# Two-block transformer kernel: seven early modulation products moved from TensorE to VectorE, and the start of the first projection reordered

## The chip, the cores and the metric

The kernel runs on one core of one Trainium2 chip. The metric is the device time of one execution in microseconds (us), lower is better. Before the change it is 2683.89 us, the median of three runs (2682.54 to 2684.22).

## The reference, cut to what matters

Two transformer blocks run one after the other on x of 256 tokens by 2048 features, all in float32. The change touches only the beginning of the first block, the modulation that comes from a conditioning vector c:

```python
c_act = jax.nn.silu(c)                         # (1, 2048)
mod = c_act @ w_ada[l] + b_ada[l]              # w_ada is 2048 x 12288
sh1, sc1, gt1, sh2, sc2, gt2 = jnp.split(mod, 6)
h = rms_norm(x, g_norm1) * (1 + sc1) + sh1
proj = h @ w_in[l]                             # first projection
```

`c_act @ w_ada` is a product of one row with a large matrix: there is little arithmetic in it, and 100 MB of weights to load. `sh1` and `sc1` are needed before the first projection can be multiplied, for each block of 128 features of h.

## The kernel before, in words

**Weights and units.** A weight load brings 512 rows by 512 columns (1 MB) into one of four `raw` buffers. Each load is used in two units (`DU`), 1024 values per partition each. For a unit, ScalarE copies its half of the load to `w_hi` in the reduced format fp32r (L1135), VectorE subtracts that from the original into `w_lo` (L1657), and TensorE makes 12 matmuls of 128x512 (L632): hi times hi, lo times hi, hi times lo, over two blocks of features and two blocks of tokens. Both helper engines run a `split` ahead of TensorE: at unit u they split unit u + 3 (`AHEAD` is 3). `w_hi` and `w_lo` have four buffers (`SPL`), so that ScalarE's split of unit u waits for TensorE's unit u - 4.

**Modulation loads.** The products with `w_ada` that feed `sh1` and `sc1` come in 32 loads of 1 MB (`NPRO`), numbered a = 0 to 31, called p0 to p31 here as products and e0 to e31 as loads. They go through a ring of four buffers of their own (`PRO_RING`): two in `early_mix`, two in `wide`. p0 to p15 (`LEAD` is 16) form two groups of eight, and are multiplied before unit 0, in `prologue()`; they give the first eight blocks of features. p16 to p31 form four groups of four loads: sh1 and sc1 for blocks 8 to 11 (p16 to p19, p20 to p23), and for blocks 12 to 15 (p24 to p27, p28 to p31). Every product is four TensorE matmuls (L662) whose stationary operand is 32 columns of `ccol`, of which the first holds silu(c) and the rest are zero. The sums of a group gather in a PSUM bank, VectorE copies them to `part` (L1708, or L1703 for the first two groups), TensorE adds up the partitions with a column of ones (`part_columns`, L679, L676 for the first two), and VectorE adds the bias and the gain (L1726, L1730, L1733). When sh1 and sc1 of a segment are there, ScalarE scales the transposed x (L1254) and VectorE splits it in `actT_hi` and `actT_lo` (L1910, L1911, the function `modulated`), two blocks of features at a time; q0 to q7 name these pieces. TensorE's unit u of the first eight needs piece q = u for u up to 3, with every piece shared by the three output groups.

**Order.** Every engine runs a program of its own in a fixed order. `prologue()` lists the steps before unit 0; before the change they end with products p16 and p17. `modulation(u)` lists what follows unit u: first the columns of the group that the product before finished, then the product p(17 + u), for u from 1 to 14. VectorE does in its unit u: `split` of unit u + 3, attention stages, then the events of `modulation(u)`, then pieces of h. So anything that VectorE does for p(17 + u) stands behind its split of unit u + 3, and that split stands behind the arrival of the weight load of unit u + 3. The columns of a group come behind unit 3 (p16 to p19), 7, 11 and 15.

**Queues.** SyncE issues all the weight loads in order. After each of the first eight projection loads w0, w1, ... it issues two modulation loads (w0, e16, e17, w1, e18, e19, ...). A modulation load waits until the product four before it has been made (`early_ada`, L485): for TensorE's product that is the semaphore `ada_used`, or `part_ready` when it was the last of its group. A projection load waits until the split of the load four before it is made (L455). GpSimd's queue waits for all six groups (`part_ready` at 6) and then loads the table of attention biases, 1.5 MB, over the two ring buffers in `wide` (L1614). TensorE turns that table with matmuls at L779 (`mirror`), the first behind unit 17.

Of the kernel before, what the change touches and what calls it, by code (L numbers as in the profile page):

```python
# [9 lines left out]
ALU = mybir.AluOpType  # L10
# [7 lines left out]
NW = 512  # L18
UC = 2
DU = 2  # L20
RAW = 4
SPL = 4
AHEAD = 3
# [40 lines left out]
LEAD = 2 * SEGMENTS[0][1]  # L64
NPRO = 32
PRO_RING = 4
# [12 lines left out]
LOAD_OF = [(g, r) for g, (kind, k0, n) in enumerate(GROUPS) for r in range(n)]  # L79
# [5 lines left out]
def last_of_group(a):  # L85

    return LOAD_OF[a][1] == GROUPS[LOAD_OF[a][0]][2] - 1


def completed(a):  # L90

    if a < WIDE:
        return [LOAD_OF[a][0]] if last_of_group(a) else []
    return [len(GROUPS) + (a - WIDE) // 4] if a % 4 == 3 else []


def sums_by(a):

    if a < NPRO:
        return LOAD_OF[a][0] + 1  # L100
    return len(PROLOGUE) + ((a - NPRO) // 2 + 1 if a < WIDE else (WIDE - NPRO) // 2 + a + 1 - WIDE)
# [8 lines left out]
def prologue():  # L110

    steps = [("diagonal",)]
    for a in range(LEAD):
        steps.append(("part", a))
        if a >= 1:
            steps += [("columns", n) for n in completed(a - 1)]
        if 5 <= a < 13:
            steps.append(("x", 2 * (a - 5)))
        if a == 13:
            steps.append(("gains",))  # L120
        if a == 14:
            steps.append(("rows",))
    steps += [("columns", n) for n in completed(LEAD - 1)]
    return steps + [("part", LEAD), ("part", LEAD + 1)]


def modulation(u):

    def products(v):

        after = [0, 1] if v == 0 else [v // DU + 1]
        return [NPRO + LOADS_A.index(k) for j in after if v >= 0 and v % DU == 0 and j < len(LOADS_W) - 1
                for k in range(LOADS_W[j] + 1, LOADS_W[j + 1])]

    def early(v):

        return [LEAD + 1 + v] if 0 < v < NPRO - LEAD - 1 else []
    events = [("row", n) for a in products(u - 3) for n in completed(a) if n >= len(GROUPS)]  # L140
    events += [("columns", n) for a in products(u - 2) for n in completed(a)]
    events += [("columns", n) for a in early(u - 1) for n in completed(a)]
    return events + [("part", a) for a in early(u) + products(u)]


def takes_bank(what, n_):

    return what != "part" or (NPRO <= n_ < WIDE and n_ % 2 == 0) or (LEAD <= n_ < NPRO and LOAD_OF[n_][1] == 0)


def banks_of(u):

    return len([1 for e in modulation(u) if takes_bank(*e)])
# [49 lines left out]
def build(nc, A, out, scr_bias, scr_x):  # L203
    ctx = ExitStack()
    with ctx:
        def sb(name, shape, dt=F32, c=ctx):
            return c.enter_context(nc.sbuf_tensor(name, shape, dt))

        def sem(name):
            return ctx.enter_context(nc.semaphore(name))  # L210
# [38 lines left out]
        part = sb("part", [P, NW])  # L249
# [17 lines left out]
        ccol = sb("ccol", [P, DC, 32])  # L267
# [27 lines left out]
        early = [early_mix[:, 0, :], early_mix[:, 1, :], wide[:, 0, :], wide[:, 1, :]]  # L295
# [12 lines left out]
        early_in = [sem(f"early_in{i}") for i in range(PRO_RING)]  # L308
# [30 lines left out]
        part_ready = sem("part_ready")  # L339
# [6 lines left out]
        c_ready = sem("c_ready")  # L346
        col_ready = sem("col_ready")
        ada_used = sem("ada_used")
        lam_exp = sem("lam_exp")
        xb_in = sem("xb_in")  # L350
        gt_in = sem("gt_in")
# [83 lines left out]
        def _(sp):  # L435
# [36 lines left out]
            def early_ada():  # L472

                a = asked[0]
                asked[0] += 1
                if a >= PRO_RING:
                    used = a - PRO_RING
                    if used < LEAD:
                        sp.wait_ge(ada_used, used + 1)
                    elif last_of_group(used):  # L480
                        sp.wait_ge(part_ready, sums_by(used))
                    else:
                        sp.wait_ge(ada_used, used + 1 - (LOAD_OF[used][0] - 2))
                view, width = columns_of(a)
                sp.dma_start(early[a % PRO_RING].rearrange("p (k n) -> p k n", n=width), view) \  # L485
                    .then_inc(early_in[a % PRO_RING], 16)
# [116 lines left out]
        def _(pe):  # L603
# [38 lines left out]
            def part_sums(a):  # L642


                if a < NPRO:
                    src = early[a % PRO_RING]
                    pe.wait_ge(early_in[a % PRO_RING], 16 * (a // PRO_RING + 1))
                else:
                    ld = LOADS_A[a - NPRO]
                    src = raw[:, ld % RAW, :]  # L650
                    pe.wait_ge(raw_in[ld % RAW], L.landed(ld))
                g, r = LOAD_OF[a]
                n_ = GROUPS[g][2]
                if a < LEAD:
                    dst = acc[2][:, g, :]
                begins, ends = (r == 0, r == n_ - 1) if a < NPRO else (a % 2 == 0, a % 2 == 1)
                if a >= LEAD:
                    if begins:
                        opened[0], _ = wait_bank()
                    dst = bank[opened[0]]  # L660
                for j in range(4):
                    ins = pe.matmul(dst[32 * j:32 * j + 32, :], ccol[:, 2 * r + j // 2 if n_ == 8 else 4 * r + j, :],  # L662
                                    src[:, j * NW:(j + 1) * NW], start=begins, stop=ends)
                if a >= LEAD and ends:
                    ins.then_inc(bank_full[opened[0]], 1)
                elif a < NPRO:
                    ins.then_inc(ada_used, 1)
# [95 lines left out]
            b, _ = wait_bank()  # L763
# [130 lines left out]
            for w in range(24, 28):  # L894
# [3 lines left out]
                m = L.n[("acc", pair)]  # L898
# [5 lines left out]
                for c in range(2):  # L904
                    for t in range(TT):
                        for s, (x, wt) in enumerate(((0, w_hi), (0, w_lo), (1, w_hi))):
                            ins = pe.matmul(acc[pair][:, t, :], MIXT[x][:, 12 + c, t * P:(t + 1) * P],  # L907
                                            wt[:, (u0 + c) % SPL, p * NW:(p + 1) * NW], start=c == 0 and s == 0,
                                            stop=c == 1 and s == 2)
# [732 lines left out]
        def _(dve):  # L1642
            L = Ledger()

            def link(ins):

                ins.then_inc(dch, 1)
                dve.wait_ge(dch, L.next("dch"))

            def split():  # L1650

                u = L.n.get("split", 0)
                if u >= UNITS:
                    return
                ld = LOADS_W[u // DU]
                dve.wait_ge(hi_ready, L.next("split"))
                dve.tensor_tensor(w_lo[:, u % SPL, :], raw[:, ld % RAW, (u % DU) * 1024:(u % DU + 1) * 1024],  # L1657
                                  w_hi[:, u % SPL, :].bitcast(F32), ALU.subtract).then_inc(lo_ready, 1)
# [34 lines left out]
            def part_sums(a):  # L1693

                g, r = LOAD_OF[a]
                if takes_bank("part", a):
                    opened[:] = L.n["bank"] % 2, L.n["bank"] // 2 + 1
                    L.n["bank"] += 1
                if (a < NPRO and not last_of_group(a)) or (a >= NPRO and a % 2 == 0):
                    return  # L1700
                if a < LEAD:
                    dve.wait_ge(ada_used, a + 1)
                    ins = dve.tensor_copy(part[:, :], acc[2][:, g, :])  # L1703
                else:
                    b = opened[0]
                    dve.wait_ge(bank_full[b], opened[1])
                    if a < NPRO or r == 1:
                        ins = dve.tensor_copy(part[:, :], bank[b][:, :])  # L1708
                    else:
                        ins = dve.tensor_tensor(part[:, :], part[:, :], bank[b][:, :], ALU.add)  # L1710
                ins.then_inc(part_ready, 1)
                dve.wait_ge(part_ready, sums_by(a))
                if a >= LEAD:
                    dve.sem_inc(bank_free[b], 1)
# [157 lines left out]
            for c in range(4):  # L1872
                ins = dve.memset(sel[32 * c:32 * c + 32, c % 2:c % 2 + 1], 1.0)
            link(ins)
            b = next_bank()
# [3 lines left out]
            b = next_bank()  # L1879
# [35 lines left out]
            def turned():  # L1915
# [3 lines left out]
            todo_of = {"part": part_sums, "columns": part_columns, "diagonal": lambda: diagonal(inv_rms()),  # L1919
                       "x": lambda k: turned(), "gains": gain_columns, "rows": second_rows}  # L1920
            for s in prologue():
                if s[0] in todo_of:
                    todo_of[s[0]](*s[1:])
            for _ in range(DU):
                split()
            modulated(0)
            for _ in range(AHEAD - DU):
                split()
            for q in pieces_of(1)[1:]:
                modulated(q)  # L1930
# [177 lines left out]
            for g in range(4):  # L2108
# [12 lines left out]
                for t in range(TT):  # L2121
                    ins = dve.tensor_tensor(s3[:, t, :], s3[:, t, :], grow[:, cols], ALU.mult)
# [276 lines left out]
            r = x_inv_rms()  # L2399
            link(dve.tensor_copy(r_mlp, r[:, 0:TT]))  # L2400
            dve.sem_inc(r_last, 1)
            for t in range(TT):
                dve.scalar_tensor_tensor(out=x_res[:, t, 3 * NW:D], in0=x_res[:, t, 3 * NW:D], scalar=r_mlp[:, t:t + 1],
                                         in1=grow[:, 3 * NW:D], op0=ALU.mult, op1=ALU.mult).then_inc(y_ready, 1)
# [50 lines left out]
```

## Time and profile before

| what | value |
|---|---|
| median of three runs | 2683.89 us (2682.54 to 2684.22) |
| the profiled execution's own time | 2680.39 us |
| span of its trace | 2678.6 us |
| TensorE matmuls busy | 2604.9 us, 97% of the span, 12160 matmuls |
| VectorE busy | 1549.4 us, 58% |
| ScalarE busy | 1167.9 us, 44% |
| DMA | 561.73 MB, mean 210 GB/s, 391 and 379 GB/s in the first two fortieths |
| granted TensorE clock, whole span | 0.991 of full speed |

The time outside the span is 1.8 us. The matmul ends in this profile are modelled and overlap each other, so that a busy share near 100% says that TensorE had a matmul in flight, not that it ran at its peak. Starts are the better measure: the distance between the first matmuls of two units is what a unit costs.

### The profile page before, as it was taken

Reading aid. Unit: us, or ns where it says so; the run is one execution under the profiler, and the core shown is the slowest. Engines: PE = TensorE matmul, PEld = TensorE weight load, DVE = VectorE, ACT = ScalarE, POOL = GpSimd, SP = SyncE. Lnnn points to the kernel's source line nnn. Section 1 sums busy time; section 2 is a strip of 40 time slices with the busy share of each in tenths; the row PEclk is TensorE's granted clock in tenths of the full one; section 3 lists DMA queues with packets and bytes.
Section 4 is the critical chain, followed back from the end, with each engine's and each line's share of the span. In section 5 each row is a group of like instructions: output and inputs, shape, how many; then the busy total and the mean of one; then the engine's idle time right before and its main releaser. Section 6 shows DMA issues by size and latency. Waiting matters only on the chain.

```text
span 2678.6 us, 32964 instructions
## 1 busy us (share of the span) xinstructions
PE 2604.9 (97%) x12160; PEld 2084.3 (78%) x12160; DVE 1549.4 (58%) x1706; ACT 1167.9 (44%) x1522; POOL 53.5 (2%) x86
## 2 busy tenths in 40 slices
PE   6999989899999999999999999999999999999997
PEld 2676766688888888887888877888888888888886
DVE  1456654667776555557655454556556565656565
ACT  2344553344434444444544445444444444444443
POOL 1010110000000000000000000000000000000000
PEclk8999999999999999999999999999999999999999
DMA  9967766657776555555655544656565555555553
GB/s 391 379 235 283 259 252 220 219 194 244 244 245 233 189 188 188 189 192 170 218 189 187 173 144 145 205 202 217 189 203 189 188 188 188 188 188 188 189 187 109
DMA packets 262882, 561.73 MB, mean 210 GB/s; under 512 B 9250, under 2 KB 13556, under 8 KB 261900
## 3 DMA queue, kind: packets, MB, share of 16 engines
q1 hardware_dynamic: 260688, 549.25, 60.6%
q0 software_dynamic: 1728, 9.19, 1.0%
q10 hardware_dynamic: 380, 2.13, 0.2%
q8 instruction: 56, 0.92, 0.1%
q14 instruction: 30, 0.25, 0.0%
HBM read 556.32 MB, written 4.21 MB: 209 GB/s over the span
## 4 chain that ended last, share of the span: by engine, by line
PE 83%; DVE 2%; ACT 1%; issue 1%; DMA 0%; POOL 0%; DVEq 0%; POOLq 0%; ACTq 0%
PE acc L632 78%; PE bank L715 2%; PE bank L662 1%; PE bank L864 1%; DVE w_lo L1657 0%; PE acc L855 0%; PE acc L1064 0%; PE acc L854 0%; PE acc L1063 0%; PE acc L907 0%; PE bank L727 0%; DMA raw<-in_w_ada 0%; PE bank L689 0%; DVE wide L2173 0%; DVE x_res L2177 0%
## 5 line engine op out<-in xcount | busy, mean ns | idle before, releaser
L1657 DVE TENSOR_TENSOR w_lo<-raw,w_hi 128x1024 fp32r<-128x1024 f32 x852 | 1037.9, 1225 | 828.6 <-ACT w_hi L1135 799.9
L1135 ACT ACTIVATE w_hi<-raw 128x1024 fp32r<-128x1024 f32 x852 | 901.2, 1060 | 1063.2 <-PE acc L632 958.6
L632 PE MATMUL acc<-w_hi,actT_hi 128*128 128x512 f32 (+1 forms) x2112 | 832.7, 394 | 1.4 <-DVE actT_lo L1792 1.0
L632 PE MATMUL acc<-w_hi,actT_lo 128*128 128x512 f32 (+1 forms) x2112 | 820.9, 389 | 0.0
L632 PE MATMUL acc<-w_lo,actT_hi 128*128 128x512 f32 (+1 forms) x2112 | 820.3, 388 | 0.0
L632 PE MATMUL acc<-w_hi,mixT_hi 128*128 128x512 f32 (+1 forms) x1280 | 504.4, 394 | 8.8 <-DVE mixT_lo L1782 4.3
L632 PE MATMUL acc<-w_hi,mixT_lo 128*128 128x512 f32 (+1 forms) x1280 | 499.1, 390 | 0.0
L632 PE MATMUL acc<-w_lo,mixT_hi 128*128 128x512 f32 (+1 forms) x1280 | 498.3, 389 | 0.0
L632 PEld LDWEIGHTS acc<-w_hi,actT_hi 128*128 128x128 f32 x2112 | 397.1, 188 | 106.3 <-issue 20.0
L632 PEld LDWEIGHTS acc<-w_hi,actT_lo 128*128 128x128 f32 x2112 | 396.9, 188 | 82.5
L632 PEld LDWEIGHTS acc<-w_lo,actT_hi 128*128 128x128 f32 x2112 | 397.3, 188 | 79.3 <-issue 1.0
L632 PEld LDWEIGHTS acc<-w_hi,mixT_hi 128*128 128x128 f32 x1280 | 241.4, 189 | 69.4 <-issue 11.4
L632 PEld LDWEIGHTS acc<-w_hi,mixT_lo 128*128 128x128 f32 x1280 | 241.4, 189 | 49.6
L632 PEld LDWEIGHTS acc<-w_lo,mixT_hi 128*128 128x128 f32 x1280 | 241.8, 189 | 47.6
L2150 DVE TENSOR_TENSOR x_res<-x_res,acc 128x1024 f32<-128x1024 f32 x68 | 83.1, 1221 | 30.4 <-PE acc L632 30.4
L662 PE MATMUL bank<-raw,ccol 128*32 128x512 f32 x384 | 47.2, 599 | 6.4 <-DMA raw<-in_w_ada 4.0
L715 PE MATMUL bank<-cst,work 128*128 128x128 f32 x356 | 47.7, 273 | 5.5 <-DVE att L2013 2.5
L2150 DVE TENSOR_TENSOR wide<-wide,acc 128x1024 f32<-128x1024 f32 x36 | 44.0, 1221 | 14.5 <-PE acc L632 14.5
L1183 ACT ACTIVATE mixT_hi<-bank 128x512 fp32r<-128x512 f32 (+1 forms) x54 | 25.6, 503 | 61.2 <-PE bank L715 37.4
L715 PEld LDWEIGHTS bank<-cst,work 128*128 128x128 f32 x356 | 41.6, 140 | 13.7 <-DVE att L2013 2.9
L1439 ACT ACTIVATE work<-acc,kpe 128x512 f32<-128x512 f32 x48 | 30.4, 686 | 39.3 <-PE acc L632 39.3
L1686 DVE SCALAR_TENSOR_TENSOR part<-raw,ccol,part 128x512 f32<-128x512 f32 x60 | 45.1, 751 | 1.7
(269 smaller groups left out, 1063.1 us busy)
## 6 DMA issues: line engine op xcount, KB each, us to landing
raw<-in_w_ff SPq DMA_DIRECT2D x128, 1024.0 KB, 5.1
raw<-in_w_in SPq DMA_DIRECT2D x108, 1024.0 KB, 5.1
raw<-in_w_ada SPq DMA_DIRECT2D x64, 1024.0 KB, 5.2
raw<-in_w_gate SPq DMA_DIRECT2D x44, 1024.0 KB, 5.0
raw<-in_w_up SPq DMA_DIRECT2D x44, 1024.0 KB, 5.1
raw<-in_w_down SPq DMA_DIRECT2D x44, 1024.0 KB, 5.0
early_mix<-in_w_ada SPq DMA_DIRECT2D x16, 1024.0 KB, 9.2
wide<-in_w_ada SPq DMA_DIRECT2D x16, 1024.0 KB, 8.9
```

The costliest lines, as they stand in the source:

```text
L632: last_mm = pe.matmul(acc[p][:, t, 0:width], act[x][:, k0 + c, t * P:(t + 1) * P], w[:, u % SPL, c * NW:c * NW + width], start=first and c ...
L662: ins = pe.matmul(dst[32 * j:32 * j + 32, :], ccol[:, 2 * r + j // 2 if n_ == 8 else 4 * r + j, :], src[:, j * NW:(j + 1) * NW], start=beg ...
L715: ins = pe.transpose(bank[b][:, j * P:(j + 1) * P], src_of(j), ident)
L864: ins = pe.matmul(bank[b][:, 0:S], v[:, k, h * P:(h + 1) * P], attT[:, k, :], start=(k == 0), stop=(k == 1))
L1135: act.activation(w_hi[:, u % SPL, :], raw[:, ld % RAW, (u % DU) * 1024:(u % DU + 1) * 1024], ACT.Copy) \
L1183: act.activation(dst, bank[b][:, 0:n], ACT.Copy).then_inc(bank_hi, 1)
L1439: ins = act.activation(stg[:, t * NW:(t + 1) * NW], acc[p][:, t, :], ff, scale=scale[:, t:t + 1])
L1657: dve.tensor_tensor(w_lo[:, u % SPL, :], raw[:, ld % RAW, (u % DU) * 1024:(u % DU + 1) * 1024], w_hi[:, u % SPL, :].bitcast(F32), ALU.subt ...
L1686: ins = dve.scalar_tensor_tensor(out=part[:, :], in0=src, scalar=ccol[:, k, 0:1], in1=part[:, :], op0=ALU.mult, op1=ALU.add)
L2150: link(dve.tensor_tensor(dst[:, :, g * NW:(g + 1) * NW], dst[:, :, g * NW:(g + 1) * NW], acc[g % 2][:, :, :], ALU.add))
```

## The change

Three things are done.

- **Seven products go to VectorE.** The second and third product of each of the four groups of four, except p17, are made on VectorE: p18, p21, p22, p25, p26, p29 and p30. Each is four instructions over 128x512: the load's quarter times a column of `ccol`, added to `part`. The first of a group's VectorE products begins with a plain `tensor_scalar`, which sets `part`; the others are `scalar_tensor_tensor`. TensorE makes the first and the last product of a group in its bank (and p17), and when the last is made, VectorE adds the bank to `part` instead of copying it. A new semaphore `dve_used` tells SyncE that a load multiplied on VectorE can be overwritten.
- **p17 is moved** from before unit 0 to behind unit 0.
- **The first split on VectorE is moved** ahead of the columns of the second group (the last thing that unit 0 waits for), and the second split behind the first piece of h, which it stood ahead of.

```diff
@@ prologue
     steps += [("columns", n) for n in completed(LEAD - 1)]
-    return steps + [("part", LEAD), ("part", LEAD + 1)]
+    return steps + [("part", LEAD)]
@@ modulation
-        return [LEAD + 1 + v] if 0 < v < NPRO - LEAD - 1 else []
+        return [LEAD + 1 + v] if 0 <= v < NPRO - LEAD - 1 else []
...
+def on_dve(a):
+
+    return LEAD + 1 < a < NPRO and LOAD_OF[a][1] in (1, 2)
+
+
+def released_by(a):
+
+    if last_of_group(a) and a >= LEAD:
+        return "part_ready", sums_by(a)
+    return ("dve_used" if on_dve(a) else "ada_used",
+            len([b for b in range(a + 1) if on_dve(b) == on_dve(a) and not (b >= LEAD and last_of_group(b))]))
@@ SyncE, early_ada
-                    used = a - PRO_RING
-                    if used < LEAD:
-                        sp.wait_ge(ada_used, used + 1)
-                    elif last_of_group(used):
-                        sp.wait_ge(part_ready, sums_by(used))
-                    else:
-                        sp.wait_ge(ada_used, used + 1 - (LOAD_OF[used][0] - 2))
+                    name, m = released_by(a - PRO_RING)
+                    sp.wait_ge({"part_ready": part_ready, "ada_used": ada_used, "dve_used": dve_used}[name], m)
@@ TensorE, part_sums
+                if on_dve(a):
+                    return
@@ VectorE, part_sums
+                if on_dve(a):
+                    dve.wait_ge(early_in[a % PRO_RING], 16 * (a // PRO_RING + 1))
+                    for j in range(4):
+                        src, col = early[a % PRO_RING][:, j * NW:(j + 1) * NW], ccol[:, 4 * r + j, 0:1]
+                        if j == 0 and not on_dve(a - 1):
+                            ins = dve.tensor_scalar(part[:, :], src, col, None, ALU.mult)
+                        else:
+                            ins = dve.scalar_tensor_tensor(out=part[:, :], in0=src, scalar=col, in1=part[:, :],
+                                                           op0=ALU.mult, op1=ALU.add)
+                        link(ins)
+                    dve.sem_inc(dve_used, 1)
+                    return
...
-                    if a < NPRO or r == 1:
+                    if a >= NPRO and r == 1:
                         ins = dve.tensor_copy(part[:, :], bank[b][:, :])
                     else:
                         ins = dve.tensor_tensor(part[:, :], part[:, :], bank[b][:, :], ALU.add)
@@ VectorE, before unit 0
             for s in prologue():
+                if s == ("columns", 1):
+                    split()
                 if s[0] in todo_of:
                     todo_of[s[0]](*s[1:])
-            for _ in range(DU):
-                split()
             modulated(0)
-            for _ in range(AHEAD - DU):
+            for _ in range(AHEAD - 1):
                 split()
```

## Rows read from the trace of the kernel before

**Rows 1.** Windows: instructions busy by engine, granted clock, DMA share, GB/s.

```profile
51.00:53.00 2.00, 1.09 (x8) 0.20 (x8) 0.82 (x4) 0.00 (x0) 0.00 (x0) 0.69 1.05 409
...
100.00:110.00 10.00, 10.00 (x52) 6.39 (x50) 5.61 (x9) 4.67 (x5) 0.00 (x0) 1.00 1.05 401
```

**Rows 2.** Waits of TensorE from 60 to 150 us: total, times, longest.

```profile
PE bank L662 <- DMA early_mix<-in_w_ada: 0.6, 1, 0.6
```

**Rows 3.** ScalarE's timeline: start, duration, instruction, count, idle before and its releaser.

```profile
57.29 1.09 ACT L1254 ACTIVATE xT<-xT,mcol 128x256 f32<-128x256 f32 x2 [0.81 <-DVEq L1742]
...
77.68 2.01 ACT L1135 ACTIVATE w_hi<-raw 128x1024 fp32r<-128x1024 f32 x2 [5.73 <-DMA raw<-in_w_in]
...
95.89 2.08 ACT L1254 ACTIVATE xT<-xT,mcol 128x256 f32<-128x256 f32 x4 [1.73 <-DVEq L1742]
...
108.54 1.06 ACT L1135 ACTIVATE w_hi<-raw 128x1024 fp32r<-128x1024 f32 x1 [3.67 <-DMA raw<-in_w_in]
...
117.05 1.06 ACT L1135 ACTIVATE w_hi<-raw 128x1024 fp32r<-128x1024 f32 x1 [5.79 <-DMA raw<-in_w_in]
```

**Rows 4.** TensorE's timeline at the start of unit 0 and of unit 1.

```profile
59.60 1.94 PE L662 MATMUL bank<-early_mix,ccol 128*32 128x512 f32 x8 [0.61 <-DMA early_mix<-in_w_ada]
61.47 0.79 PE L632 MATMUL acc<-w_hi,actT_hi 128*128 128x512 f32 x1
...
65.45 0.39 PE L632 MATMUL acc<-w_hi,actT_hi 128*128 128x512 f32 x1
...
66.15 0.39 PE L632 MATMUL acc<-w_hi,actT_hi 128*128 128x512 f32 x1
...
68.99 1.07 PE L662 MATMUL bank<-wide,ccol 128*32 128x512 f32 x8
```

**Rows 5.** TensorE's timeline, first matmuls of units 4 and 5, and the columns.

```profile
76.80 0.95 PE L679 MATMUL bank<-ones,part 128*128 128x1 f32 x8
...
78.67 0.50 PE L632 MATMUL acc<-w_hi,actT_hi 128*128 128x512 f32 x1
...
82.61 0.50 PE L632 MATMUL acc<-w_hi,actT_hi 128*128 128x512 f32 x1
...
93.37 0.95 PE L679 MATMUL bank<-ones,part 128*128 128x1 f32 x8
...
109.94 0.95 PE L679 MATMUL bank<-ones,part 128*128 128x1 f32 x8
...
126.51 0.95 PE L679 MATMUL bank<-ones,part 128*128 128x1 f32 x8
132.90 1.02 PE L779 MATMUL bank<-wide,att 128*128 128x512 f32 x2
```

**Rows 6.** VectorE's timeline at the first units.

```profile
59.62 0.42 DVE L1910 CAST actT_hi<-xT 128x512 fp32r<-128x512 f32 x1
...
65.07 0.69 DVE L1911 TENSOR_TENSOR actT_lo<-xT,actT_hi 128x512 fp32r<-128x512 f32 x1
...
71.03 2.36 DVE L1657 TENSOR_TENSOR w_lo<-raw,w_hi 128x1024 fp32r<-128x1024 f32 x2 [2.00 <-ACT w_hi L1135]
```

**Rows 7.** VectorE's timeline where it makes other modulation products later on.

```profile
588.88 0.48 DVE L1684 TENSOR_SCALAR part<-raw,ccol 128x512 f32<-128x512 f32 x1
...
591.85 2.36 DVE L1657 TENSOR_TENSOR w_lo<-raw,w_hi 128x1024 fp32r<-128x1024 f32 x2
594.12 3.11 DVE L1686 SCALAR_TENSOR_TENSOR part<-raw,ccol,part 128x512 f32<-128x512 f32 x4
```

**Rows 8.** DMA issues by tile: count, KB each, median us from issue to landing.

```profile
raw<-in_w_in SPq DMA_DIRECT2D x108, 1024.0 KB, 5.1
...
wide<-in_w_ada SPq DMA_DIRECT2D x8, 1024.0 KB, 8.9
```

**Rows 9.** The load of the bias table: its issue, and its time to landing.

```profile
124.78 1.00 POOL L1614 DMA_DIRECT2D wide<-bias_by_distance  x1 [103.49 <-DVE part L1708]
...
DMA to landing us min/median/max: 7.7/7.7/7.7
```

More of the change, by code:

```diff
@@ L348, in build @@
         ada_used = sem("ada_used")
+        dve_used = sem("dve_used")
         lam_exp = sem("lam_exp")
```

## Prediction, made before the changed kernel was run

> **What bounds the kernel now.** The whole program is bound by TensorE, but the change acts only in the first 135 us, so I read that stretch alone, first by windows. While the 32 modulation loads run, TensorE has work in flight all the time and the DMA engines are also full, with a share of 1.05 [rows 1]. Two things are at their limit together, and the question is which one is just ahead. TensorE's waits say that TensorE is the later: from 60 to 150 us it waited 0.6 us in all [rows 2]. ScalarE's timeline shows the other side: its `w_hi` waits for the arrival of weights, at 77.68 and 108.54, four loads later, so a projection load and its two modulation loads arrive every 7.72 us, 2.57 us each [rows 3]. TensorE's starts give its own beat: unit 1 takes 68.99 - 66.15 = 2.84 us [rows 4], unit 4 with p21 behind it 82.61 - 78.67 = 3.94, so a product costs 1.10, and columns come every 16.57 us or four units (93.37, 109.94, 126.51) [rows 5], 8.28 per pair of units. TensorE is thus only 0.56 us per pair slower than the DMA, and its data lie ready a little longer with each pair.
>
> **What the change removes.** Seven products at 1.10 us make 7.7 us off TensorE. If nothing else bound it, that would be the gain.
>
> **The start.** Before: unit 0 begins at 61.47, when p17 is through [rows 4]. After: p16 ends at 59.60 - 0.61 = 58.99 [rows 4], ScalarE has piece q0 at 57.29 + 1.09 = 58.38 [rows 3], and VectorE splits it in 0.42 + 0.69 [rows 6] right then, since two w_lo splits no longer stand ahead (now it starts at 59.62, behind them). Unit 0 starts at about 59.6, 1.8 us earlier. The split moved ahead of the columns costs nothing: it runs beside TensorE's column matmuls, and if it came late the columns would be late by a part of its 1.2 us. But unit 1 needs q1, whose lo part ends at 65.07 + 0.69 = 65.76 [rows 6]: it comes behind ScalarE's copy of the second load, which waits for DMA, and nothing in the change moves it. Unit 0 at the slow clock takes some 4.7 us, p17 1.1, and unit 1 starts at 65.85 against 66.15. The start gives 0.3 us; p17 is hidden in the gap. Unit 2 would follow p18 at 69.98; without p18 it starts at 68.65, unit 3, behind p19, at 72.5, and TensorE wants the first columns at 75.3.
>
> **What VectorE adds, and where it stands.** A group's first VectorE product takes 591.85 - 588.88 = 2.97 us, the other, all `scalar_tensor_tensor`, 3.11 and a link, 3.2; a split 1.15, half the step from 591.85 to 594.12 [rows 7]; the add of the bank 0.69, as the copy before it and as the tensor_tensor of its shape [rows 6]. Four of the one and three of the other: 21.5 us on an engine that is busy for 5.6 us in ten there [rows 1]. In sum there is room. In order there is less: VectorE's product behind unit u stands behind its split of unit u + 3, that waits for the weight's arrival, and the group's columns on TensorE wait for all of it. Followed group by group (each time is the one before it plus a duration above; a load's split starts 1.1 us behind its arrival):
>
> - *First columns.* Split of unit 4 at 71.03 as now [rows 6], p18 72.2 to 75.15, split of unit 5 to 76.35, add to 77.05. Columns at 77.15, against 76.80 before [rows 5]. TensorE waits 1.8 us: the gain is gone, +0.35.
> - *Second.* TensorE goes on from 77.15, skips p21 and p22 and wants the columns at 91.45. VectorE: p21 81.5 to 84.5; the next load arrives at 77.68 + 7.72 = 85.4, its split ends 87.65; p22 to 90.85, split to 92.0, add to 92.7. Columns at 92.8 against 93.37: -0.55.
> - *Third.* TensorE wants them at 107.15. VectorE: ScalarE's pieces q4 and q5 go ahead of its next copy as now, 95.89 to 97.97 [rows 3], so the split of unit 11 ends at 100.1; p25 to 103.1, pieces q4, q5 to 105.4, split of unit 12 to 106.55, p26 to 109.8, split to 110.95, add to 111.65. Columns at 111.75 against 109.94: +1.8, and TensorE has waited 4.6 us.
> - *Fourth.* TensorE wants them at 111.75 + 1.87 + 2.84 + 2.84 + 3.94 + 2.84 = 126.1. Here the ring matters. SyncE may issue e29 only when p25 is made, 103.1, against about 99 now, and e30 when p26 is, 109.8 against 103. A load takes at least 5.1 us from issue to landing [rows 8]. e29 lands at 108.3, 2.4 us behind its place in the queue, w7 at 110.9 (now 108.54), e30 at 114.9, e31 at 117.4, w8 at 120 (now 117.05 [rows 3]). Splits of unit 16 to 122.3, p30 to 125.5, split to 126.65, add to 127.35. Columns at 127.45 against 126.51: +0.95.
>
> *A page's figure for that latency.* The Trainium skill, DMA: Bandwidth & Descriptors, section on the anatomy of one DMA, has a fixed part of about 2.0 us and the bytes at 436 GB/s. That would be 4.4 us for 1 MB in place of the row's 5.1, and the fourth columns 0.7 us earlier, a minor shift, but on its side the late release costs less.
>
> **What is late last.** GpSimd loads the bias table when all groups are made: 124.78 now [rows 9], some 2.9 us later after, 127.65. It takes 7.7 us to land [rows 9], so 135.4. TensorE's first matmul on it stands at 132.90 now [rows 5], in the same microsecond in which the table lands (124.78 + 7.7 = 132.5). After, TensorE would be there at 127.45 + 0.82 + 2 x 2.84 = 133.9 and wait for the table to 135.4: **+2.5 us**. Beyond that TensorE is bound by itself, nothing gives slack back, and the shift reaches the end. The other end of this case: if the ring's late releases cost nothing, w8 arrives as now, the sixth group is done at 124.5 and the table at 132.5, so -0.4; if each is late by another microsecond, +4.
>
> Sum: 2680.39 + 2.5 = 2682.9 for an execution like the profiled one, which lies 3.5 us under the median of 2683.89; put to the median, 2686.4. A difference of this kernel under about 0.2% (5.4 us) can't be told from no change.
>
> **Rivals.**
>
> 1. *The gain is whole.* If VectorE is never what the columns wait for, TensorE has 7.7 + 0.3 = 8.0 us less: 2675.9. For it: VectorE's busy share, and that TensorE is the later now. Against: the DMA is only 0.56 us per pair behind it, and the order above. Chance 0.05.
> 2. *Waits and covers come out even.* The columns wait less than I count (a link is cheaper, a load comes a little earlier), and the table lands as now. Then the time is that of the table's landing, between 0 and 3 us less: 2682.5. Chance 0.21.
> 3. *The DMA queue runs dry* (slower). Place: SyncE's wait for `dve_used`, with w7, e30, e31 and w8 queued behind it. It decides if a load released late needs not 5.1 but the 8.9 us that ring loads take now [rows 8]. Then e29 lands at 112, w7 114.6, e30 118.7, w8 123.8, p30 is made at 130.2, the last add ends at 132, the table lands at 140: +7.1, 2691.0. For: the DMA is full, other loads stand ahead. Against: the 8.9 is mostly queue, and a late release is late because the queue is empty. Chance 0.12.
> 4. *The clock falls in the new waits.* At 51 to 53 us, with TensorE idle between small products, the granted clock goes to 0.69 of full on the mean, the lower of its levels (1.2 of 2.4 GHz) for part of it [rows 1]; in unit 0 nine matmuls take 65.45 - 61.47 = 3.98 us instead of 2.1 [rows 4] until it is back. A wait of 4.6 us could do the same: 1.9 us a time. Behind the third columns the fourth wait (1.35 us) and that for the table (1.5 us) take this up; only if it happens at two or more of the waits does it show, +2 to +4 on the forecast, 2689.5. Chance 0.07.
>
> The Trainium skill, TensorE: Matmul & The Clock Gate, section on why this matters for your kernels, warns of just such idle gaps between bursts of matmuls, as dropping the clock to half. By that rule the fourth rival would happen at least at the third columns; the trace has such a drop only at 51 us.
>
> **How the numbers follow.** The forecast, +2.5 us, has 0.55; the rivals 0.05, 0.21, 0.12 and 0.07. Forecast alone: 2683.5 to 2688. The range of 8 in 10 takes in the second and fourth and most of the third: 2680 to 2691. Faster by over 0.2%: the first rival and a little of the second, 0.06. Slower by over 0.2% (over 2689.3): two thirds of the third, a third of the fourth, 0.10. Within 0.2%: 0.84.
>
> **What would show it.** TensorE's waits, 60 to 150 us, should have columns (L679 before) waiting for VectorE's add of the bank: 1.8, 1.4, 4.6 and 1.4 us. Unit 0 should start near 59.6 and unit 1 near 65.8. SyncE should wait for the products on VectorE, and the DMA share should have a dip near 104 us. The first L779 matmul should start near 135.4, right after the table's landing, and everything later keep that distance. The prediction is wrong if that matmul starts before 130 (then VectorE and DMA had slack I did not see) or after 138, or if a shift made here changes again later, for instance through a wait at a modulation load in the attention stages.

## The result, and the profile after

The changed kernel takes 2690.82 us, the median of nine runs (2688.91 to 2695.24), beside 2682.72 us for the kernel before (nine runs, 2681.04 to 2685.63). The ratio is 1.0031, 95% interval 1.0022 to 1.0040: slower by about 8 us, where the forecast was 2.5 us slower and 0.84 of the chance lay within 5.4 us of no change. The profiled execution of the changed kernel is at its median (span 2688.8 us); that of before was 2.3 us under what is now the median of before, so the two spans differ by 10.2 us and the times by 8.1.

TensorE's timeline of the changed kernel, at the rows that answer to [rows 4, 5]; an idle time before the row and its releaser stand in brackets:

```profile
59.67 0.79 PE L641 MATMUL acc<-w_hi,actT_hi 128*128 128x512 f32 x1 [0.71 <-DVE actT_lo L1934]
...
66.28 0.50 PE L641 MATMUL acc<-w_hi,actT_hi 128*128 128x512 f32 x1
...
76.92 1.05 PE L690 MATMUL bank<-ones,part 128*128 128x1 f32 x8 [0.96 <-DVE part L1733]
...
94.09 1.05 PE L690 MATMUL bank<-ones,part 128*128 128x1 f32 x8 [1.19 <-DVE part L1733]
...
113.08 1.68 PE L690 MATMUL bank<-ones,part 128*128 128x1 f32 x8 [3.02 <-DVE part L1733]
...
130.45 0.95 PE L690 MATMUL bank<-ones,part 128*128 128x1 f32 x8
139.64 1.14 PE L790 MATMUL bank<-wide,att 128*128 128x512 f32 x2 [2.64 <-DMA wide<-bias_by_distance]
```

The start is as forecast, 1.8 us earlier for unit 0 and nothing for unit 1. The matmuls on the columns (L690, four times) stand 0.1, 0.7, 3.1 and 3.9 us later than before, the first matmul on the bias table 6.7 us later. TensorE waits at three of the columns, for VectorE's add of the bank, and at the table; at the fourth columns, where 1.4 us were forecast, it does not wait. VectorE's timeline in front of the first columns shows what stands in one row behind an arrival: a split, p18, a split, the add.

```profile
70.91 1.23 DVE L1668 TENSOR_TENSOR w_lo<-raw,w_hi 128x1024 fp32r<-128x1024 f32 x1 [2.13 <-ACT w_hi L1146]
72.05 0.48 DVE L1712 TENSOR_SCALAR part<-wide,ccol 128x512 f32<-128x512 f32 x1
72.57 2.33 DVE L1714 SCALAR_TENSOR_TENSOR part<-wide,ccol,part 128x512 f32<-128x512 f32 x3
75.04 1.22 DVE L1668 TENSOR_TENSOR w_lo<-raw,w_hi 128x1024 fp32r<-128x1024 f32 x1
76.18 0.68 DVE L1733 TENSOR_TENSOR part<-part,bank 128x512 f32<-128x512 f32 x1
```

The weight loads show where the extra lateness comes from. SyncE's timeline (start, time, issue, count) and ScalarE's (`w_hi` behind the arrivals of w3, w4 and w8):

```profile
74.98 2.28 SPq L494 DMA_DIRECT2D wide<-in_w_ada  x2
77.31 0.51 SPq L469 DMA_DIRECT2D raw<-in_w_in  x1
79.03 5.58 SPq L494 DMA_DIRECT2D early_mix<-in_w_ada  x2
...
111.14 2.28 SPq L494 DMA_DIRECT2D wide<-in_w_ada  x2
```

```profile
77.53 2.00 ACT L1146 ACTIVATE w_hi<-raw 128x1024 fp32r<-128x1024 f32 x2 [5.71 <-DMA raw<-in_w_in]
86.72 2.01 ACT L1146 ACTIVATE w_hi<-raw 128x1024 fp32r<-128x1024 f32 x2 [7.18 <-DMA raw<-in_w_in]
...
122.88 2.22 ACT L1146 ACTIVATE w_hi<-raw 128x1024 fp32r<-128x1024 f32 x2 [8.24 <-DMA raw<-in_w_in]
```

e22 could be issued at 74.98 only (70.1 before), when p18 was made on VectorE. Behind it stood e23, which waits for the group's sum: the two issues together last till 77.26, past VectorE's add at 76.18. By their times to landing e22 arrives at 80.8, 0.6 us later than before, and e23 at 84.2, 1.4 us later: most of the lateness of w4, the load behind them, comes with e23. Between w3 and w4 now lie 9.2 us; the beat before was 7.72 [rows 3]. w5, w6 and w7 arrive 1.6, 2.6 and 4.1 us later than before, and w8 at 122.88 against 117.05, 5.8 us. The table follows:

```profile
130.50 1.00 POOL L1625 DMA_DIRECT2D wide<-bias_by_distance  x1 [109.77 <-DVE part L1733]
...
DMA to landing us min/median/max: 9.1/9.1/9.1
```

And three windows in which TensorE waited or ran at the lower clock, their entries in the order of [rows 1]:

```profile
70.00:80.00 10.00, 9.04 (x48) 5.71 (x47) 7.00 (x9) 3.83 (x4) 0.00 (x0) 0.96 1.02 356
...
110.00:120.00 10.00, 6.98 (x25) 4.57 (x25) 8.02 (x11) 2.00 (x2) 0.00 (x0) 0.67 0.96 331
...
140.00:150.00 10.00, 10.00 (x33) 7.10 (x32) 2.65 (x3) 4.35 (x6) 0.00 (x0) 0.83 0.51 177
```

The DMA moves 356 GB/s at 70 to 80 us and 331 at 110 to 120, where it moved 408 and 400. The granted clock falls behind each of TensorE's four waits in the rows above: 0.67 of full on the mean at 110 to 120, 0.83 at 140 to 150. The step on GpSimd that stood at 142.70 before stands at 151.12, 8.4 us later: 6.7 from the table and 1.7 from the clock behind it. From that step to the end of the span it is 2535.9 us before and 2537.7 here. Among the traces of the experiments this remainder goes from 2536.1 to 2542.1, so a single span says little about a few us.

### The profile page after: what moved, and what is told of

It reads as the page before. It is cut to its first block, busy times and chain, and to the rows that moved or that the text cites. A ratio compares the mean times of both kernels' runs of the same rounds, so it can differ in the third digit from the quotient of the medians.

```text
span 2688.8 us, 32887 instructions
## 1 busy us (share of the span) xinstructions
PE 2608.4 (97%) x12104; PEld 2089.2 (78%) x12104; DVE 1568.3 (58%) x1734; ACT 1167.6 (43%) x1522; POOL 54.0 (2%) x86
## 4 chain that ended last, share of the span: by engine, by line
PE 89%; DMA 4%; DVE 4%; ACT 2%; issue 1%; POOL 0%; SPq 0%; DVEq 0%; POOLq 0%; ACTq 0%
PE acc L641 82%; PE bank L726 2%; DMA raw<-in_w_in 2%; PE bank L673 1%; DMA wide<-in_w_ada 1%; DMA raw<-in_w_ada 1%; DVE w_lo L1668 1%; PE bank L875 1%; ACT w_hi L1146 1%; DVE part L1714 0%; PE acc L866 0%; PE acc L1075 0%; DMA wide<-bias_by_distance 0%; PE acc L865 0%; PE acc L1074 0%
```

## The experiments

Every version was run beside the kernel before on the same chip, 5 to 11 times. The ratio to the kernel before has its 95% interval in brackets; 0.001 is 2.7 us. The changed kernel stands at 1.0031. "At 143 us" is the lateness of GpSimd's first step behind the modulation stage, against the trace of before. Such a lateness, like every start quoted below, is from one execution per version. "..." marks what a diff leaves out.

### Which part of the change

**The start alone.** `on_dve` is false for all, and the last product's sum is copied as before.

```diff
-    return LEAD + 1 < a < NPRO and LOAD_OF[a][1] in (1, 2)
+    return False
```

> Only the new start: p17 behind unit 0, first split ahead of the columns; all 32 products on TensorE. Theory A (VectorE's order and the ring's late releases cause the loss): the start is worth nothing, unit 1 begins near 66.2 as in both kernels, and the time is that of before, 2682.7 within 1 us. Rival B (the start itself costs, because e21 is issued 4 us later and everything behind it in SyncE's queue with it): the DMA share dips near 75 us and the time is 2684.5 to 2687.

Measured: 1.0002 (0.9993 to 1.0012), +0.3 at 143 us, w4 at 85.13, w8 at 117.22. The later issue of e21 costs nothing.

**The products alone.** The start of before (p17 ahead of unit 0, two splits behind the columns), the seven products on VectorE.

```diff
-    return steps + [("part", LEAD)]
+    return steps + [("part", LEAD), ("part", LEAD + 1)]
...
-        return [LEAD + 1 + v] if 0 <= v < NPRO - LEAD - 1 else []
+        return [LEAD + 1 + v] if 0 < v < NPRO - LEAD - 1 else []
```

> Only the seven products on VectorE, with the start of before. Theory A: nearly the whole loss, 2689 to 2692, first columns at 76.9 us, first matmul on the bias table near 139.5. Rival B (the start is to blame for a good part): 2684 to 2687.

Measured: 1.0031 (1.0018 to 1.0043), first matmul on the table at 141.21, w8 at 124.47. The whole loss is in the products.

### Order, amount of work, release

**The product ahead of the split.** Same work, other order in VectorE's unit.

```diff
             def unit(todo=()):
+                events = modulation(L.n.get("unit", 0))
+                for e in events:
+                    if e[0] == "part" and e[1] < NPRO and on_dve(e[1]):
+                        part_sums(e[1])
                 split()
...
```

> The changed kernel, but VectorE makes its product of a unit ahead of that unit's split instead of behind it. Same work, same engines, other order. Theory A: p18 is made from 68.8 to 71.8 in a gap, e22 is issued at 71.8 instead of 75, no columns wait but the third (3.7 us), the table is issued near 123 and the first matmul on it is near 131.4 (before: 132.9, changed: 139.6): 2680.5 to 2683. Rival E (it is VectorE's amount of work or the port to its memory, not the order): 2688 to 2691.

Measured: 0.9996 (0.9987 to 1.0005), no loss left; the interval lies wholly under that of the changed kernel. VectorE's timeline and ScalarE's:

```profile
69.10 0.48 DVE L1718 TENSOR_SCALAR part<-wide,ccol 128x512 f32<-128x512 f32 x1
69.61 2.33 DVE L1720 SCALAR_TENSOR_TENSOR part<-wide,ccol,part 128x512 f32<-128x512 f32 x3
72.09 2.36 DVE L1668 TENSOR_TENSOR w_lo<-raw,w_hi 128x1024 fp32r<-128x1024 f32 x2
```

```profile
85.35 2.01 ACT L1146 ACTIVATE w_hi<-raw 128x1024 fp32r<-128x1024 f32 x2 [5.69 <-DMA raw<-in_w_in]
...
117.35 1.06 ACT L1146 ACTIVATE w_hi<-raw 128x1024 fp32r<-128x1024 f32 x1 [6.89 <-DMA raw<-in_w_in]
```

p18 is made in a gap in which VectorE waited for a load; e22 goes out at 72.03, and w4 and w8 come when they came before. VectorE makes as many products, for as long each, so neither its amount of work nor a slower access to its memory was the loss. TensorE still waits 3.3 us at the third columns (108.41), and the first matmul on the table is at 132.25, forecast 131.4. At 143 us this version is 0.5 us early.

**Work on VectorE that nobody reads.** All products are TensorE's, and VectorE does the same 28 instructions on constants in the same places.

```diff
+                    idle = probs[:, 0:2, :].rearrange("p a s -> p (a s)")
...
+                            ins = dve.tensor_scalar(idle, src, col, None, ALU.mult)
...
+                            ins = dve.scalar_tensor_tensor(out=idle, in0=src, scalar=col, in1=idle,
...
```

> The new start, all 32 products on TensorE with the ring released by TensorE, and on VectorE, in the places of the seven products, the same 28 instructions on constants and a scratch tile, whose result nobody reads. It holds VectorE's order alone, without late releases and without TensorE's gain. Theory A: the third columns are 1 to 2 us late, loads keep their 7.7 us beat (arrivals of w4 and w8 near 85.4 and 117.2), time 1 to 2.5 us over the kernel before: 2684.5 to 2686. Rival F (VectorE's order is most of the loss, the ring little): 2688 to 2691.

Measured: 1.0014 (1.0005 to 1.0022), 3.8 us, more than forecast. w4 at 85.77 and w8 at 119.85: the beat was not kept to the end. What is late in this version too is VectorE's copy of a group's sum, which releases the group's last buffer; that this is the cause was not tried by itself. At 143 us +3.6.

**The same, with the late release.** SyncE waits for VectorE's place too.

```diff
+                    if late(a - PRO_RING):
+                        sp.wait_ge(dve_used, len([b for b in range(a - PRO_RING + 1) if late(b)]))
```

> As the run with idle products, but SyncE waits in addition for VectorE's place before it reuses the buffer, as in the changed kernel. The difference to that run is the late release alone. Theory A: w4 arrives near 86.8 to 88.5 and w8 near 122 to 124, the table is issued near 130.5, time 6 to 9 us over the kernel before, 2689 to 2692. Rival F: within 1.5 us of the run with idle products.

Measured: 1.0021 (1.0012 to 1.0029), 1.9 us over the one before by the ratios, whose intervals overlap. Its one trace has w4 at 87.03, w8 at 123.41, the table at 140.02 and +8.9 at 143 us; it belongs to the slowest of its eleven runs, and behind 143 us that run is another 4.2 us longer than the trace of before. The arrivals show the mechanism; how many us the release alone costs stays between 2 and 5.

**Four products instead of seven**, in the changed kernel's order.

```diff
+    return LEAD + 1 < a < NPRO and LOAD_OF[a][1] in (1, 2) and a not in (22, 26, 30)
```

> The changed kernel in its own order, but only one product of a group on VectorE (p18, p21, p25, p29); p22, p26, p30 back on TensorE. Theory A (two products, a split between them, and the add in one chain behind each load's arrival): only p18 is still in the way, w4 arrives near 86.7, but the second to fourth columns no longer wait; the table is issued near 124.5 and the time is that of before within 1.5 us. If the loss goes by the number of products: 4/7 of 8 us, 2688 to 2689.

Measured: 1.0013 (1.0004 to 1.0022), +3.5 us, under the 4/7 of the loss but not the zero that I forecast. The columns do come back, 94.15, 110.36 and 125.81 (before: 93.37, 109.94, 126.51). But w4 at 87.40 and w8 at 121.70 stay late, and the table, issued at 126.05, is used at 135.72 after a wait of 3.29 us. The columns were not the whole path.

### The clock

**Idle matmuls in the waits.** TensorE multiplies constants into the bank that the next real matmul overwrites, once with 2, 2, 6 and 5 of them and once with 1, 1, 3 and 3.

```diff
+                if n_ in WARM:
+                    b, _ = wait_bank()
+                    for _ in range(WARM[n_]):
+                        pe.matmul(bank[b][:, :], ident, cst[:, 0:NW], start=True, stop=True)
                 pe.wait_ge(part_ready, L.value("groups", sums_of(n_), 4))
...
```

> The changed kernel with idle matmuls (identity times constants, into the bank that the next real matmul overwrites) in front of the columns' and the table's waits: 2, 2, 6 and 5 of them, about 0.5 us each, so that TensorE is busy while it waits. Theory A: the waits stay, the granted clock stays at full, and only the half-clock stretch behind the last wait (the table's) and part of that behind the third columns come off the end: 1.5 to 3.5 us less than the changed kernel, 2687.3 to 2689.3. Rival C (the clock is the loss, the waits by themselves are covered): 2683 to 2685. Rival D (the clock costs nothing at the end): 2690 to 2692.

Measured: 1.0041 (1.0027 to 1.0054). The matmuls took 0.86 us each, not 0.5, ran past the waits, and made all later. The try had no verdict on the clock.

> The changed kernel with idle matmuls again, but cut to the waits that its own trace shows: 1, 1 and 3 ahead of the first three columns and 3 ahead of the table (0.86 us each, as measured in the first try, where they ran past the waits and made everything later). If the half-clock stretches are part of the loss at the end: full clock from 70 to 150 us, first matmul on the table still near 139.6, everything behind it 1.7 us earlier than in the changed kernel, 2687.5 to 2690 where the changed kernel gives 2691. If they are not: 2690.5 to 2692.5.

Measured: 1.0037 (1.0024 to 1.0051), beside 1.0031 (1.0018 to 1.0043) for the changed kernel, run again beside it:

> The changed kernel once more, beside the others on the same chip, as what they are compared with: 7.5 to 9 us over the kernel before, first matmul on the table 6.5 to 8.5 us later than in the kernel before.

TensorE's windows with idle matmuls (busy, granted clock, DMA share, GB/s):

```profile
80.00:90.00 10.00, 10.00 (x48) 1.00 1.04 385
90.00:100.00 10.00, 8.40 (x43) 1.00 1.01 351
...
110.00:120.00 10.00, 7.26 (x25) 0.69 0.94 326
120.00:130.00 10.00, 10.00 (x47) 0.97 1.00 385
130.00:140.00 10.00, 9.98 (x43) 1.00 0.83 287
140.00:150.00 10.00, 9.74 (x37) 1.00 0.56 188
```

The clock stays up at the first, second and last wait, of which 0.79, 1.60 and 0.28 us were left, and falls at the third, where 2.74 us were left. The columns stand where they stood (93.76, 113.45, 130.86), and at 143 us the kernel is 7.5 us late; the repeated changed kernel, whose wait at the table was 0.87 us in that execution, is 7.4 late. So here a half-clock stretch ahead of another wait cost nothing that shows, and the one behind the table is there in some executions only: in the repeated one the clock fell behind a wait of 1.82 us at the fourth columns instead. I have no gain from a kept clock to show. In both versions' traces the excess over the changed kernel arises behind 143 us (6.2 and 5.3 us more than in the trace of before, against 1.8 for the changed kernel); why is open.

### The table

**Its use one unit later.**

```diff
-            todo = {-7: [("mirror", 0)], -6: [("mirror", 1)], -5: [("qk", 0), ("mirror", 2)], -4: [("mirror", 3)],
+            todo = {-6: [("mirror", 0)], -5: [("qk", 0), ("mirror", 1)], -4: [("mirror", 2)],
...
```

> The changed kernel with each of the six steps on the bias table one unit later. Theory A: TensorE has unit 18 to do while the table arrives at 139.6, so the wait of 2.7 us goes, and with it the stretch at half the clock (1.7): 4 us less than the changed kernel, 2686 to 2688. Rival G (the shift is made before the table, by the columns): no more than 1 us less.

Measured: 1.0023 (1.0014 to 1.0032), 2 us less than the changed kernel. At 143 us it is 5.0 late instead of 8.4, but behind the attention stages, at GpSimd's step that stood at 380.68 before, 9.0 where the changed kernel is 9.8. Why most of the gain goes again between was not found.

**Its load issued by SyncE**, behind w9, instead of by GpSimd.

```diff
+                    if n[0] == 10 and i is None:
+                        sp.wait_ge(brow_out, 16)
+                        sp.wait_ge(part_ready, len(PROLOGUE))
+                        sp.dma_start(biasE, bass.AP(scr_bias.tensor, 0, [[1, P], [512, H], [1, 384]])) \
+                            .then_inc(bias_in, 16)
...
-            pool.wait_ge(part_ready, len(PROLOGUE))
-            pool.dma_start(biasE, bass.AP(scr_bias.tensor, 0, [[1, P], [512, H], [1, 384]])).then_inc(bias_in, 16)
```

> The changed kernel with only the table's load moved to SyncE behind w9. If the table's landing is a term of its own in the loss: it lands near 137 instead of 139.6, TensorE does not wait for it nor drop its clock behind it, 3 to 4.4 us less than the changed kernel, 2686 to 2688. If the shift is all made by the columns and releases ahead of it: no more than 1 us less, 2690 to 2691.

Measured: 1.0021 (1.0012 to 1.0030), 2.7 us less by the ratios, whose intervals overlap; at 143 us the kernel is 5.7 late instead of 8.4, the same 2.7. The table lands in 6.4 us and TensorE uses it at 138.55 without a wait. Taken so, the table is a term of its own, about a third of the loss, and two thirds are made ahead of it. The edit does one thing more: SyncE now waits for the sixth group before it issues w10, and the DMA is at 158 GB/s from 120 to 130 us, where it was at 366; TensorE does not wait for a weight load behind it.

### What the idea is worth

**All modulation events ahead of the split**, in VectorE's units 0 to 14.

```diff
             def unit(todo=()):
-                split()
+                ahead = L.n.get("unit", 0) <= 14
+                if not ahead:
+                    split()
...
+                if ahead:
+                    split()
+                    run(todo)
```

> The changed kernel, but in VectorE's units 0 to 14 all that belongs to the modulation (products, the add of the bank, the columns) stands ahead of the split. Theory A: the third columns move from 108.4 (products alone ahead) to about 107, the fourth to about 121.5, the table is issued near 119 and the first matmul on it is near 128: 2678 to 2680.5, 4 to 5 us under the kernel before. Rival H (a split that stands behind TensorE's product now holds up a unit, or the loads' beat is what ends last): 2682 to 2685.

Measured: 0.9992 (0.9983 to 1.0001). Third and fourth columns at 106.61 and 122.40, table used at 129.56, 3.2 us early at 143 us. That trace is of the shortest of its eleven executions; the ratio stands for about 2 us, half of the 4 to 5 forecast. TensorE still waits 3 us at the third columns.

**The same with five products**, p26 and p30 back on TensorE.

```diff
-    return LEAD + 1 < a < NPRO and LOAD_OF[a][1] in (1, 2)
+    return LEAD + 1 < a < NPRO and LOAD_OF[a][1] in (1, 2) and a not in (26, 30)
```

> The version with all modulation events ahead of the split, and p26 and p30 given back to TensorE, so that VectorE makes five products. In the version with seven TensorE waited 3 us at the third columns. Here that wait should go for 1.1 us of matmuls, and the third columns come near 105, the table is issued near 118.5, first matmul on it near 127.5: 1 to 2 us under the version with seven, 2677 to 2680.5. If the loads' beat or the table ends last in both, no difference: 2680 to 2682.

Measured: 0.9992 (0.9983 to 1.0001), no further gain, and the trace shows why. TensorE's timeline:

```profile
104.59 0.95 PE L690 MATMUL bank<-ones,part 128*128 128x1 f32 x8
...
119.94 0.95 PE L690 MATMUL bank<-ones,part 128*128 128x1 f32 x8
129.80 2.07 PE L790 MATMUL bank<-wide,att 128*128 128x512 f32 x2 [3.32 <-DMA wide<-bias_by_distance]
```

No columns wait any more, the fourth come at 119.94, 6.6 us earlier than before [rows 5]. The table is issued at 119.51, but now takes 10.2 us, with weight loads of SyncE in flight beside it (one issued about 4 us ahead of it, one about 1 us behind). TensorE waits 3.3 us, its clock is at 0.71 in the window from 130 to 140 us, and at 143 us the 6.6 us are 0.1. This trace is of one of the two longest executions of eleven, 4.7 us over their median, and behind 143 us it is 5.1 us longer than that of before, so it shows where the gain can go, not how much goes on the mean.

**Five products, the table used later**, by the diff of "Its use one unit later".

> The five-product version with each step on the bias table one unit later. If the table alone ate its gain: TensorE does unit 18 while the table lands at 129.8, no wait over 0.6 us, full clock, everything behind it 4 to 5 us earlier than in the kernel before, 2677 to 2679 where that has 2682. If something else catches up behind 140 us (as in the changed kernel with the later use, where half of the 4 us went again): 2680 to 2681.5.

Measured: 0.9981 (0.9972 to 0.9990), 2677.22 us beside 2682.41. At 143 us it is 5.8 us early.

**Five products, the table by SyncE**, by the diff of "Its load issued by SyncE", without the later use.

> The five-product version, with the table's load issued by SyncE behind w9 instead of by GpSimd behind everything queued. The table lands 6.5 to 7 us after its issue at 119.5, at 126 to 126.5, just as TensorE comes for it: first matmul on it near 126.5, 6 us earlier than before, 2676 to 2678.5 if w10 and w11, now behind the table, still come in time; 2679 to 2682 if they don't.

Measured: 0.9977 (0.9968 to 0.9986), 2676.22 us beside 2682.41: faster than both kernels, by 6 us than the one before, and at 143 us 5.8 us early. The two ways of moving the table can't be told apart, and their intervals still overlap that of five products with the table as it was (0.9983 to 1.0001). TensorE's timeline and the table's time to landing:

```profile
126.65 1.02 PE L795 MATMUL bank<-wide,att 128*128 128x512 f32 x2
130.68 1.02 PE L795 MATMUL bank<-wide,att 128*128 128x512 f32 x2
```

```profile
DMA to landing us min/median/max: 6.3/6.3/6.3
```

## Why the prediction was right and wrong

**The start: right.** Unit 0 began at 59.67 (forecast 59.6). Unit 1 began at 66.28, 0.1 us later than before and 0.4 later than the forecast 65.85, since unit 0 took 5.4 us at the lower clock and not the 4.7 of before. The run with the start alone gave no difference.

**The mechanism: right.** The chain behind a load's arrival (split, product, split, product, split, add, columns) is what TensorE waits for: 0.96, 1.19 and 3.02 us at the first three columns, forecast 1.8, 1.4 and 4.6. The run with the same work in another order shows that the order is the cause. VectorE's products were as costed: from the start of one to the start of the split behind it, 2.99 and 3.26 us, forecast 2.97 and 3.2.

**The size: wrong.** +2.5 us were forecast and 8.1 measured. The direction was right and the median lay just inside the range, which ended at 2691, but that range was built on a median of 2683.89 for the kernel before, which is 2682.72 beside the changed kernel; and slower by over 0.2%, which is what came (0.31%), had been given a chance of 0.10. The likeliest case was mis-sized in three terms:

- *The ring.* I let only e29 and e30 be late and kept w4 at 85.4. The step that failed is "the next load arrives at 77.68 + 7.72 = 85.4": it prices VectorE's late release of e22 at nothing. I had also not counted that e23 waits for the buffer of p19, the last product of its group, which VectorE's add releases, now behind a product and a split, and that w4 is next in SyncE's queue. w4 came at 86.72 and w5 behind it at 94.70, against 93.10; the second columns (94.09, forecast 92.8) and the third (113.08, forecast 111.75) were each 1.3 us later than forecast. At the fourth group, e30 went out at 111.14, not 109.8, and from there w8 took 11.7 us, not 10.2: e31 too could go out only behind VectorE's add (113.03), and landed 4.0 us behind e30, not 2.57. So w8 came at 122.88, forecast 120, and the table was issued at 130.50, forecast 127.65: 2.85 us.
- *The table's landing.* It took 9.1 us, not 7.7: 1.4 us. I took one row's duration as a constant, though that load shares the DMA engines with others. The two terms are the difference at the table, 2.5 + 2.85 + 1.4 = 6.7.
- *The clock.* The fourth rival had 0.07. The granted clock fell behind the waits at all three columns and at the table, already behind a wait of 1 us, where I had asked for one of 4.6. That the trace of before has such a drop only at 51 us holds for the stretch that I had read: it has others later, 0.58 of full at 365 to 370 us, 0.62 at 525 to 530 and 0.66 at 1260 to 1265. A short wait does not always do it either: the clock stayed at full behind waits of 1.42 and 2.34 us at the third columns of the two runs with idle products on VectorE. Behind the table it cost 1.7 us in this execution, since no wait follows there to cover it: 8.4 at 143 us, beside 8.1 between the medians. How often it falls there is open; in the repeated run it did not, and the time was the same within a microsecond.

The slow rival, the DMA queue running dry, had 0.12, and its 2691.0 is the measured time to 0.2 us. That is luck. Its place was right, loads did come late one after the other behind the wait for `dve_used`. Its condition was not met: it wanted 8.9 us from issue to landing for a load released late, and e26, e29 and e30 took 5.2, 5.2 and 5.1, e22 5.8, close to the forecast's 5.1 (the 4.4 that the prediction sets beside this was too short for these loads of SyncE). w8 came 2.9 us over the forecast's 120 by late issues, where the rival had 3.8, and the rest is the table and the clock. Its sum has a slip too: from w8 at 123.8 to the last add the forecast's own steps take 7.35 us, which gives 131.2 and not 132, and 2690.1 in place of 2691.0.

The first rival, the whole gain, was not wrong in principle: with the order changed and the table out of the way, five of the products on VectorE give 6 us. As a forecast for this change it failed, by VectorE's order.

## What to carry to other kernels

In this kernel, moving work to an engine with a low busy share paid only where its place in that engine's order was free. Behind a step that waits for data, it inherits that wait, and everything that it releases (a buffer, a semaphore, the next load in an in-order queue) is late by it. So put it ahead of the waiting step, into the gap. And before crediting a gain, look for the next event that is already tied with the path, here a 1.5 MB load that landed within half a microsecond of its use: it can take most of a gain until it is moved too.

## What the runs showed of the hardware

- The granted clock could fall to 0.50 of full after a wait of TensorE of about 1 us between units. In the changed kernel TensorE waited 0.96 us, made the eight small matmuls of the columns in the next 1 us, then the eight of p20 at full clock, and was at half from 79.2 us on: eight matmuls with starts 0.43 us apart until 82.6. Behind waits of 1.19 (five products, table later), 1.60 (fitted idle matmuls) and 2.34 us (idle products with the late release) the clock stayed at full, and no run here tells the cases apart. Single windows of the changed kernel:

```profile
76.00:78.00 2.00, 1.08 (x12) 1.00 0.97 248
78.00:80.00 2.00, 2.00 (x11) 0.80 1.09 344
80.00:82.00 2.00, 2.00 (x6) 0.50 0.96 331
```

- The time from issue to landing of the same 1.5 MB load was 6.3 and 6.4 us in the two kernels where SyncE issued it ahead of the next weight loads in its own queue, and 6.8 to 10.2 us in the fifteen where GpSimd issued it (6.8 with the start alone, 7.7 before, 9.1 in the changed kernel, 10.2 with five products ahead). Whether the issuing engine or the loads in flight make the difference was not tried apart.
